# V pages of a paged attention: issued by ScalarE amid its activations, not by GpSimd's loop

## The reference, cut to what matters

```python
P = page_table.shape[1] * PAGE_SIZE
past_k = pool_k[page_table].reshape(Bd, P, H_C, HEAD_DIM).astype(jnp.float32)
past_v = pool_v[page_table].reshape(Bd, P, H_C, HEAD_DIM).astype(jnp.float32)
k_all = jnp.concatenate([past_k, kc], axis=1)
v_all = jnp.concatenate([past_v, vc], axis=1)
y_c = stick_breaking(qc, k_all, v_all, b_sb, P + jnp.arange(T), jnp.arange(P + T))

def stick_breaking(q, k, v, b_sb, q_pos, k_pos):
    scale = q.shape[-1] ** -0.5
    z = jnp.einsum('bthe,bshe->bhts', q, k) * scale + b_sb.astype(jnp.float32)[None, :, None, None]
    mask = k_pos[None, :] < q_pos[:, None]
    log_stay = jnp.where(mask, jax.nn.log_sigmoid(-z), 0.0)
    later = lax.cumsum(log_stay, axis=3, reverse=True) - log_stay
    a = jnp.where(mask, jnp.exp(jax.nn.log_sigmoid(z) + later), 0.0)
    return jnp.einsum('bhts,bshe->bthe', a, v)
```

## Time and profile before

| | us |
|---|---|
| median of 3 runs | 3692.75 |
| lowest and highest | 3692.68 and 3696.47 |
| the profiled execution | 3698.46 |
| its span in the profile | 3696.6 |
| TensorE busy in the span | 3414.4 (92%) |
| VectorE busy | 2051.1 (55%) |
| ScalarE busy | 1557.1 (42%) |
| GpSimd busy | 708.9 (19%) |

### The profile page before, as it was taken

The page is one execution under the profiler, slowest core; times in us unless marked ns, Lnnn a source line. Parts: engine busy times, 40 slices in busy tenths (PEclk is TensorE's granted clock), DMA queues, the critical chain, the costliest instruction groups (busy, mean ns, idle before and its releaser), DMA issues. The chain is left out here.

```text
span 3696.6 us, 61011 instructions
## 1 busy us (share of the span) xinstructions
PE 3414.4 (92%) x21901; PEld 2934.2 (79%) x21901; DVE 2051.1 (55%) x4160; ACT 1557.1 (42%) x3055; POOL 708.9 (19%) x986
## 2 busy tenths in 40 slices
PE   8999999989996989689998979999989999899996
PEld 7999999944443665456666769999989999899996
DVE  2211134468994765436664555666666565846564
ACT  3321122268882444324443225443454344545342
POOL 0111011156671334123440120000100000200000
PEclk9999999989995989789999989999999999999998
DMA  5654456421005531678994553444443443422222
GB/s 200 219 197 164 149 180 196 150 64 44 10 10 118 109 86 41 239 266 286 356 334 142 177 173 103 143 133 139 134 157 123 134 148 127 149 81 80 69 69 77
DMA packets 435778, 533.92 MB, mean 144 GB/s; under 512 B 93701, under 2 KB 370822, under 8 KB 430502
## 3 DMA queue, kind: packets, MB, share of 16 engines
q1 hardware_dynamic: 409296, 416.94, 36.3%
q10 hardware_dynamic: 9816, 62.87, 4.9%
q0 software_dynamic: 16384, 50.35, 3.8%
HBM read 436.28 MB, written 143.91 MB: 157 GB/s over the span
## 5 line engine op out<-in xcount | busy, mean ns | idle before, releaser
L3702 PE MATMUL p_DP<-p_UH,p_WH 128*128 128x352 f32 x1536 | 500.0, 325 | 20.4 <-issue 14.2
L3703 PE MATMUL p_DP<-p_UL,p_WH 128*128 128x352 f32 x1536 | 498.6, 325 | 0.0
L3704 PE MATMUL p_DP<-p_UH,p_WL 128*128 128x352 f32 x1536 | 498.3, 324 | 0.0
L3702 PE MATMUL p_UP<-fc_TH,p_WH 128*128 128x352 f32 x1344 | 439.0, 327 | 26.8 <-DVE p_WL L3602 15.1
L3703 PE MATMUL p_UP<-fc_TL,p_WH 128*128 128x352 f32 x1344 | 436.9, 325 | 0.0
L3704 PE MATMUL p_UP<-fc_TH,p_WL 128*128 128x352 f32 x1344 | 436.7, 325 | 0.0
L964 PE MATMUL p_PP<-p_WH,p_HH 128*128 128x384 f32 (+1 forms) x1224 | 420.6, 344 | 9.2 <-DVE p_WL L640 4.8
L965 PE MATMUL p_PP<-p_WL,p_HH 128*128 128x384 f32 (+1 forms) x1224 | 409.2, 334 | 0.0
L967 PE MATMUL p_PP<-p_WH,p_HL 128*128 128x384 f32 (+1 forms) x1152 | 385.2, 334 | 0.0
L3702 PEld LDWEIGHTS p_DP<-p_UH,p_WH 128*128 128x128 f32 x1536 | 292.5, 190 | 22.5 <-issue 21.3
L3643 DVE TENSOR_TENSOR p_acc<-p_DP,p_acc 128x352 f32<-128x352 f32 x336 | 171.4, 522 | 227.3 <-PE p_DP L3704 227.3
(11 more groups left out here) (460 smaller groups left out, 6711.7 us busy)
## 6 DMA issues: line engine op xcount, KB each, us to landing
fc_WU<-in_w_up SPq DMA_DIRECT2D x48, 1024.0 KB, 5.4
p_WD<-in_w_down SPq DMA_DIRECT2D x192, 256.0 KB, 2.9
cw_K<-in_cache_sb_k SPq DMA_DIRECT2D x192, 192.0 KB, 4.2
cw_V<-in_cache_sb_v POOLq DMA_DIRECT2D x192, 192.0 KB, 5.3
out_s_wk<-in_cache_win_k ACTq DMA_DIRECT2D x64, 382.5 KB, 3.5
out_s_wv<-in_cache_win_v ACTq DMA_DIRECT2D x64, 382.5 KB, 4.1
p_HH<-scratch_xh SPq DMA_DIRECT2D x34, 512.0 KB, 4.6
p_HL<-scratch_xl SPq DMA_DIRECT2D x34, 512.0 KB, 5.4
```

The source lines that it names most:

```text
L3702: pe.matmul(out, hi, rhi, start=first, stop=False, skip_group_check=True)
L3703: pe.matmul(out, hi, rlo, start=False, stop=False, skip_group_check=True)
L3704: return pe.matmul(out, lo, rhi, start=False, stop=last, skip_group_check=True)
```

## The change

The V pages of the second to the eighth sequence are issued by ScalarE. In iteration n of ScalarE's loop, after the copy of key tile 4 of group n + 1, there follows for n = 2 to 29 a wait until `values(n - 2)` is done, the reading of the eight page numbers of group n + 2, and eight DMAs on ScalarE's hardware queue into the buffer `VP[q]` that this group uses. GpSimd's loop is gone, and with it the semaphore `passed_pool`. The V pages of the first sequence stay with GpSimd in the phase before. For the later ones there are four new semaphores `later_in`, on which TensorE waits before `values` from the second sequence on.

```diff
@@ PagedCache
         self.v_in = [m.sem(f"v_in{i}") for i in range(self.NG)]
+        self.later_in = [m.sem(f"later_in{i}") for i in range(self.NG)]
@@ stick_sample_phase
-        passed_pool = m.sem("passed_pool")
@@ gpsimd
-            with pool.Fori(1, DB) as b:
-                for q in range(NG):
-                    pages = G.pages_of(mybir.EngineType.Pool, b, q)
-                    wait_apart(pool, av_ok, b * NG + (q - NG + 1), passed_pool)
-                    G.load(pool, VP, A["cache_sb_v"], v_in, pages, q)
-
@@ scalar
                 if n + 1 < N:
                     keys(n + 1, 4)
+                if NG - 2 < n + 1 < N - 1:
+                    b, q = divmod(n + 2, NG)
+                    act.wait_ge(av_ok, n - 1)
+                    G.load(act, VP, A["cache_sb_v"], G.later_in, G.pages_of(mybir.EngineType.Activation, b, q), q)
                 if n == 0:
@@ tensor
             def values(n):
                 s, (b, q) = n % 2, divmod(n, NG)
-                pe.wait_ge(v_in[q], (b + 1) * 16 * NP)
+                if b:
+                    pe.wait_ge(G.later_in[q], b * 16 * NP)
+                else:
+                    pe.wait_ge(v_in[q], 16 * NP)
                 pe.wait_ge(a_ok, n + 1)
```

## The result

The changed kernel takes 3870.8 us (median of 4 runs, 3861.88 to 3878.64) against 3692.72 us, 1.0487 times as long (95% interval 1.0467 to 1.0507): 178.1 us slower. The forecast was 3888 us, with a range of 3800 to 3940. Its profiled execution took 3878.64 us; its span is 3876.9 us against 3696.6, 180.3 us more.

A forecast was written before the change was run, and what follows sets the result against it. TensorE, busy 92% of the span, was taken to bound the kernel. Waiting for ScalarE (129 us) plus lower clock (66 us) gave 195 us on the 3692.75 us median: 3888 us, range 3800 to 3940.

The forecast's parts named there:

- The place: TensorE's second logits block would wait for ScalarE's `ZS` copy, delayed behind the page reading and DMAs, in 28 groups.
- this hole: ScalarE's 2.65 us from the key tile 4 copy's start to the `ZS` copy's start; TensorE's slack adds 0.17 us.
- The block: ScalarE's added work per group: 2.6 us reading page numbers, 4.75 us issuing, 0.05 us handing over, 7.4 us in all.
- Rival 4: On ScalarE, the table load waits for the preceding activation: 0.58 us more a group, 3904 us; variant within the forecast's 0.80.
- The gaps: TensorE's waiting in the loop: 7.4 - 2.65 - 0.17 = 4.6 us a group, 129 us over 28 groups.
- The clock: TensorE's clock falls after each wait: 4.9 us at the lower level costs 2.35 us a group, 66 us in all.
- Rival 1: TensorE's clock stays up in the loop, leaving only 129 us of waiting: 3822 us; chance 0.10.
- rival 2: DMA issues occupy ScalarE's sequencer only briefly: 4.55 us of added work a group, 48 us in all, 3741 us; chance 0.05.
- Rival 3: ScalarE's added work fits behind the key tile 4 copy, within 2.8 us, at no cost: 3693 us; chance 0.05.
- The sum: In the loop, 129 us of waiting plus 66 us of lower clock: 195 us more, 3888 us.

The follow-up runs named there:

- the reading alone: Kernel before, V pages still issued by GpSimd, with ScalarE only reading the eight page numbers in the changed kernel's place: 3684.82 us, ratio 0.9992.
- the fitted version: Changed kernel with ScalarE's page-number reading and eight DMAs split over six places, one, one, two, one, two and one DMAs: 3688.85 us, ratio 1.0000.
- the filled gaps: Changed kernel with 32 transposes of the identity put into TensorE's order where it waits for ScalarE: 3820.06 us, ratio 1.0361.
- the run with only the issuing: Changed kernel with page numbers read once ahead of the loop, every later group issuing its eight DMAs from the same registers: 3740.35 us, ratio 1.0145.
- the spread: Changed kernel with ScalarE's work in four places, two DMAs in each, the page numbers read in the old place: 3703.57 us, ratio 1.0041.

## Why the prediction was right

- **The place.** TensorE waits at the logits for the `ZS` copy, as forecast, 28 times; the reading alone is hidden and the fitted version costs nothing, so it is the overhang over this hole that counts.
- **The block.** Forecast 7.4 us from copy to copy, measured 7.14 in the mean of 28 (6.02 to 8.24). Errors of both signs partly cancel, which is luck. From the copy to the first DMA it was 2.15 us where I had 2.8: the sequencer is ahead by one activation (the table load starts at 1791.81, 0.42 us before the copy of key tile 4 that stands ahead of it), and the reading is a little shorter than SyncE's (1.5 us from first to last assert, not 1.8). The eight issues took 4.88 us from first start to last end in the mean, against the 4.5 us between the earlier trace rows that I had taken. Rival 4, a load that waits for the activation ahead of it, did not occur.
- **The gaps.** Forecast 4.6 x 28 = 129 us, measured 119.3.
- **The clock.** Forecast 66 us from the gaps of the earlier trace rows, measured 65.5 us of longer busy time, confirmed by the filled gaps (56 us and more). Both factors fit: 4.8 us of work at the low level a group (134 us in all, which I counted from the clock's records), forecast 4.9, and 65.5 / 134 = 0.49 us lost for each, forecast 0.48. That the mean came so close is in part luck, as the three rows behind it ran from 2.78 to 6.13 us, and the same way of reckoning gave 46 us for the run with only the issuing, where 9.8 were measured. Rival 1, 129 us more, is what the filled gaps brought about: 131.5 us. The Trainium skill, "TensorE: Matmul & The Clock Gate", section "HAM oscillation — how this bites in real kernels", tells of a loop that pays in each round; the trace agrees, with 28 low stretches for 28 gaps. Its factor of one half agrees with the 0.49.
- **The rivals.** Short issues (rival 2) fail on 339 ns for the shortest of ScalarE's issues, against 332 ns for SyncE's. Rival 3, a block that fits, became true only when the block was cut up.
- **The sum.** 195 us forecast, 184.0 in the loop, 178.1 between the medians. What is missing is the 10 us of the gap term, and some 4 us outside the loop in that execution, for which no run shows a cause; the four runs of the changed kernel spread over 17 us.
- **A loose reading.** I put the V pages of the kernel before at three groups, some 26 us, ahead of use. The first of them are issued at 1691.5 us and used by the `values` block at 1723.9, four groups on and 32 us later. Nothing hangs on it: TensorE waited for no V page before or after.

Not settled is why single issues are held up (to 1.56 us on ScalarE, 1.30 us on SyncE in the same loop): no experiment took it apart. Also open is how much more each of the other places would hide: the three of the spread cost nothing, and no run looked for the limit of one of them.

## What to carry to other kernels

An engine's free share does not say what can be given to it. Find the hole in its order of work, its length from start to start and what waits behind it, and give it no more than that at once; the same readings and DMAs that cost 178 us in one piece cost nothing that could be measured in six. The gaps of 4.3 us in this TensorE-bound loop were paid half again through the clock (65.5 us on top of 119.3), and gaps of 1.5 us in the mean by a quarter (9.8 on 41.8). And before moving a load, ask who waits for it: here leaving it out altogether gained nothing.

## What the runs showed that I had not expected

ScalarE's sequencer runs ahead by one activation: what stands behind the copy of key tile 4 starts 0.42 us before this copy does. With only the issuing, 28 gaps of 1.5 us in the mean left the clock at 0.97: it fell behind four of them, of 1.97 to 2.59 us, while one of 2.03 us left it up. The few gaps of 2 to 3 us in the trace of before had made me expect a loss each time. The gaps of 4.3 us were followed by the lower level 28 times out of 28.
